# Five layer norms computed on two halves of the tokens, with the units around them split by half

## The chip, the cores and the metric

One core of a Trainium2 chip. The metric is the device time of one execution in microseconds (us). Engines: TensorE multiplies matrices into PSUM, VectorE and ScalarE work elementwise, GpSimd and SyncE issue most transfers (POOL and SP in the rows). Each engine runs its own queue in order; semaphores order the engines among each other.

## What is computed

One inference step of a decoder of 4 layers for 512 new prompt tokens and 8 sampled tokens, 1024 features wide. Layer 0 and 3 mix tokens by retention, layer 1 by pooling, layer 2 by sparse attention with an indexer. Each layer has two residual norms:

```
x = layer_norm(alpha * x + mixer(x))
x = layer_norm(alpha * x + swiglu(x))
layer_norm(x) = (x - mean) * rsqrt(var + 1e-5) * g + b        # mean and var over the 1024 features
swiglu(x)     = (silu(x @ w_a) * (x @ w_u)) @ w_out           # 2816 wide
```

## The kernel before

All 520 tokens stay on the chip with features on the partitions: `x` is 128 partitions by 8 chunks by 520 tokens. A unit is one block of 128 output features over all tokens. Its weights come from memory into one of four raw slots, ScalarE rounds them to a high part (`split_hi`, L445), VectorE takes the low part (`split_lo`, L455), and `multiply` (L471) sums three products (high by high, high by low, low by high) per 128 rows of depth, each for two halves of 260 tokens in two PSUM banks. There are two slots of split weights, so the split of unit k+2 waits until unit k is multiplied (`split_next`, L463), and two pairs of PSUM banks, so unit k+2 also waits until unit k is read out.

The stage list sets the order; each engine walks it with a program of its own. Ahead of each norm stands a stage that adds eight units to `x`: the output projection of retention (depth 4 chunks), of attention (`proj2`, depth 8) or the second part of the feed-forward output (`down..b`, depth 10). Per unit VectorE adds the product to `x`, ScalarE squares it (`square`, L950), VectorE adds value and square to two running sums (`add_up`, L1225).

The norm itself: on TensorE (L2378) mean by a product with a constant matrix (L2386), sums per token as single columns (L2392), and, after the root, a spread of 1/sd over all partitions (L2403); between them `hold` (L2372) multiplies an identity into a bank that nobody reads, 11, 10 and 13 times. On VectorE (L1812): subtract the mean (L1818), four small steps for the variance, reciprocal (L1835), scale (L1865), low part of the result (`x_lo`, L1207). On ScalarE (L1155): root (L1158), affine into `x` (L1164), high part `x_h` (L791). All of it goes chunk by chunk over all 520 tokens.

The next stage starts with two units interleaved, `multiply_first` (L500): it takes each chunk of `x_h` and `x_l` as it comes, with the second unit three chunks behind the first. Below these two are called the pair. Then the stage goes on with its third unit, called unit 2.

The norms are named by layer and place: norm0a is behind retention of layer 0, norm1b behind the feed-forward of layer 1, norm2a behind attention, norm2b behind the feed-forward of layer 2, norm3a behind retention of layer 3.

## Time and profile before

| | us |
|---|---|
| median of 3 runs (3249.36 to 3250.75) | 3249.58 |
| the profiled execution | 3249.74 |
| its span, first to last instruction | 3248.0 |
| TensorE matmul busy | 3083.2 (95%) |
| TensorE weight load busy | 2909.0 (90%) |
| VectorE busy | 1565.3 (48%) |
| ScalarE busy | 1031.9 (32%) |

Busy is the time in which an instruction of the engine was under way. Matmuls overlap each other, so the distance from one to the next, not the length of one, is what a matmul costs. A timeline row gives start, length, engine, line, operation, tiles and shapes; several instructions of one form in a row are merged, and the bracket at the end gives the idle time before and what ended it. A row of a windows view gives a stretch, its length, the busy time of each engine in it with the count of instructions, and the granted clock of TensorE as a share of 2.4 GHz.

### The profile page before, as it was taken

The page shows a single profiled execution, that of the slowest core. Times are in us where ns is not written, and L with a number is a line of the kernel's source. Part 1 is how long each engine was busy: PE and PEld are TensorE (multiplying, and loading weights), DVE is VectorE, ACT ScalarE, POOL GpSimd, SP SyncE. Part 2 cuts the span into 40 slices and gives each one's busy share as a digit, 9 for nine tenths or more (in the row PEclk, how much of TensorE's full clock was granted, in tenths as well). Part 3 has the DMA queues.
Part 4 walks back from the last instruction along what each step waited for, and adds up shares of the span by engine and source line. Part 5 has one row for each costly group of instructions (what it writes and reads, how often), then busy time and mean ns, then how long its engine had stood idle before and what let it go on. Part 6 is the DMA issues. An engine that isn't in the chain of part 4 may idle for free.

```text
span 3248.0 us, 55327 instructions
## 1 busy us (share of the span) xinstructions
PE 3083.2 (95%) x23519; PEld 2909.0 (90%) x23519; DVE 1565.3 (48%) x2423; ACT 1031.9 (32%) x1440; POOL 209.3 (6%) x342
## 2 busy tenths in 40 slices
PE   8999998999985999998898899999999999899998
PEld 7898896999985999997788799999989989699998
DVE  4555555432348332356986443234555555533234
ACT  3333332431224322232343143122523333332222
POOL 0111101000000000001011100000021011000000
PEclk9999998999996999999898899999999999899999
DMA  6444334232321332322122323233344443323231
GB/s 148 133 130 159 127 112 136 78 104 79 95 67 49 89 106 78 100 61 59 53 73 81 122 73 103 83 93 91 95 151 121 150 133 109 119 83 108 76 99 51
DMA packets 492389, 323.14 MB, mean 99 GB/s; under 512 B 29211, under 2 KB 468763, under 8 KB 492186
## 3 DMA queue, kind: packets, MB, share of 16 engines
q1 hardware_dynamic: 465394, 230.14, 24.9%
q0 software_dynamic: 26800, 90.18, 7.9%
q8 instruction: 150, 2.46, 0.3%
q14 instruction: 45, 0.37, 0.0%
HBM read 275.90 MB, written 44.82 MB: 99 GB/s over the span
## 4 chain that ended last, share of the span: by engine, by line
PE 88%; DVE 8%; ACT 2%; issue 2%; DMA 0%; POOL 0%; DVEq 0%; SPq 0%; ACTq 0%; POOLq 0%
PE ps L482 72%; PE ps L532 2%; PE ps L1900 2%; PE ps L513 2%; PE ps L533 2%; PE ps L534 2%; PE ps L2032 2%; DVE wf L1818 1%; DVE wf L1577 1%; PE ps L2022 1%; DVE tiny L1575 1%; DVE w_l L459 1%; ACT w_h L453 1%; DVE wf L1865 1%; PE ps L2336 1%
## 5 line engine op out<-in xcount | busy, mean ns | idle before, releaser
L482 PE MATMUL ps<-x_h,w_h 128*128 128x260 f32 x4576 | 936.0, 286 | 7.4 <-DVE w_l L459 5.2
L482 PE MATMUL ps<-x_h,w_l 128*128 128x260 f32 x4576 | 925.0, 284 | 0.0
L482 PE MATMUL ps<-x_l,w_h 128*128 128x260 f32 x4576 | 923.6, 284 | 0.0
L459 DVE TENSOR_TENSOR w_l<-w_raw,w_h 128x1024 fp32r<-128x1024 f32 (+3 forms) x440 | 527.9, 1200 | 817.0 <-ACT w_h L453 816.5
L453 ACT ACTIVATE w_h<-w_raw 128x1024 fp32r<-128x1024 f32 (+3 forms) x440 | 456.0, 1037 | 904.7 <-PE ps L482 874.5
L482 PEld LDWEIGHTS ps<-x_h,w_h 128*128 128x128 f32 x4576 | 710.0, 190 | 30.0 <-issue 23.7
L482 PEld LDWEIGHTS ps<-x_h,w_l 128*128 128x128 f32 x4576 | 708.6, 189 | 0.0
L482 PEld LDWEIGHTS ps<-x_l,w_h 128*128 128x128 f32 x4576 | 708.1, 189 | 0.0
L482 PE MATMUL ps<-rr,w_h 128*128 128x260 f32 x3968 | 639.4, 283 | 2.2 <-DVE w_l L459 1.1
L482 PEld LDWEIGHTS ps<-rr,w_h 128*128 128x128 f32 x3968 | 543.6, 188 | 4.1 <-issue 3.0
L482 PE MATMUL ps<-rr,w_l 128*128 128x260 f32 x1984 | 399.4, 283 | 0.0
L482 PEld LDWEIGHTS ps<-rr,w_l 128*128 128x128 f32 x1984 | 306.7, 189 | 0.0
L1790 DVE TENSOR_TENSOR wf<-ps,wf 128x520 f32<-128x520 f32 x88 | 61.5, 699 | 248.4 <-PE ps L482 248.4
L1117 ACT ACTIVATE wf<-ps 128x520 f32<-128x520 f32 x88 | 53.4, 606 | 343.7 <-PE ps L482 334.7
L532 PE MATMUL ps<-rr 128*128 128x512 f32 (+5 forms) x332 | 122.7, 372 | 7.4 <-DVE rr L1690 3.2
L1900 PE MATMUL ps<-ident,wf 128*128 128x128 f32 (+4 forms) x607 | 95.7, 290 | 35.5 <-DMA wf<-in_x_sample 9.5
L1804 DVE SCALAR_TENSOR_TENSOR x<-x,ps 128x520 f32<-128x520 f32 x40 | 27.9, 696 | 196.3 <-PE ps L482 196.3
L1900 PEld LDWEIGHTS ps<-ident,wf 128*128 128x128 f32 (+4 forms) x607 | 70.3, 142 | 56.7 <-issue 29.9
L533 PE MATMUL ps<-rr 128*128 128x512 f32 (+5 forms) x332 | 115.3, 349 | 0.0
L534 PE MATMUL ps<-rr 128*128 128x512 f32 (+5 forms) x332 | 115.1, 348 | 0.0
L1342 DVE SCALAR_TENSOR_TENSOR wf<-ps,wf 128x512 f32<-128x512 f32 x128 | 89.4, 743 | 2.5 <-ACT wf L856 2.5
L532 PEld LDWEIGHTS ps<-rr 128*128 128x128 f32 (+1 forms) x332 | 64.4, 195 | 27.6 <-issue 13.6
(278 smaller groups left out, 2765.6 us busy)
## 6 DMA issues: line engine op xcount, KB each, us to landing
w_raw<-in_ffn_w_in SPq DMA_DIRECT2D x176, 512.0 KB, 3.8
w_raw<-in_ret_w_in SPq DMA_DIRECT2D x96, 512.0 KB, 3.9
out<-wf POOLq DMA_DIRECT2D x72, 512.0 KB, 3.3
wf<-in_state_ret POOLq DMA_DIRECT2D x64, 512.0 KB, 5.6
w_raw<-in_ffn_w_out SPq DMA_DIRECT2D x32, 768.0 KB, 4.6
w_raw<-in_ffn_w_out SPq DMA_DIRECT2D x32, 640.0 KB, 4.2
w_raw<-in_ret_w_out SPq DMA_DIRECT2D x64, 256.0 KB, 2.9
w_raw<-in_dsa_w_in SPq DMA_DIRECT2D x27, 512.0 KB, 3.9
```

The costliest lines, as they stand in the source:

```text
L453: C.activation(whole(stage, k, w_h[:, n % 2, 0:m]), landed(stage, k, n, m), ACT.Copy).then_inc(S["w_hi"], 1)
L459: V.tensor_tensor(whole(stage, k, w_l[:, n % 2, 0:m]), landed(stage, k, n, m), whole(stage, k, w_h[:, n % 2, 0:m].bitcast(F32)), ALU.subtr ...
L482: mm = M.matmul(ps[:, 2 * (n % 2) + b, 0:HALF], lhs[:, c, :], rhs[:, c, cols], start=(c == 0 and term == 0), stop=(c == cs - 1 and term == 2))
L513: mm = M.matmul(ps[:, 2 * n + b, 0:HALF], lhs, rhs[:, c, cols], start=(c == 0 and term == 0), stop=(c == DC - 1 and term == 2))
L532: M.matmul(out, lhs_h, rhs_h, start=start, stop=False)
L533: M.matmul(out, lhs_h, rhs_l, start=False, stop=False)
L534: return M.matmul(out, lhs_l, rhs_h, start=False, stop=stop)
L1117: C.activation(halves(sil[:, q]), acc[0], ACT.Silu).then_inc(S["sil"], 1)
L1342: V.scalar_tensor_tensor(st[:, b % 4, d], ps[:, spread_bank(i, b), :], k_f[:, d, SEQ + b:SEQ + b + 1], st[:, b % 4, d], ALU.mult, ALU.add) ...
L1790: V.tensor_tensor(halves(h_raw[:, q]), acc[1], halves(sil[:, q]), ALU.mult).then_inc(S["h_raw"], 1)
L1900: return M.transpose(out, src, ident[0:n, 0:n])
L2032: mm = M.matmul(ps[32 * j:32 * j + 4, 6, :], qz[:, i % 2, d, g, j, :], st[:, (2 * g + j) % 4, d, :], start=(g + d == 0), stop=(g == NB // ...
```

## The change

For norm0a, norm1b, norm2a, norm2b and norm3a the norm works on two halves of 260 tokens (`norm_halves` on three engines), and it takes over the last two units of the stage ahead (units 6 and 7, counted in the eight) and the pair of the next stage.

- TensorE: unit 6 and unit 7 for the first half; unit 6 for the second half with the first half's statistics behind it or in its middle; unit 7 for the second half with the first half's spread in it or behind it; the pair for the first half, with the second half's statistics and spread between its chunks; the pair for the second half. In the pair the second unit is one group of two chunks behind the first. The `hold` products go.
- VectorE: adds and sums of units 6 and 7 by half; subtraction, scale and low part by half and two chunks at a time; the queue order is written out. The weight splits for the pair stand among the first half's steps, the second of them at their end.
- ScalarE: squares by half, two roots, per two chunks two affines into `x` and one copy into `x_h`.
- The stage ahead stops after six units, and the next stage begins with its third.

The diff, cut to its core (VectorE's and ScalarE's helpers and the semaphore counts are left out where a line of the text above says what they do):

```diff
+HALVED = {"norm0a": "sums0", "norm1b": "down1b", "norm2a": "proj2", "norm2b": "down2b", "norm3a": "sums3"}
+FOLLOWS = {"norm0a": "up0a", "norm1b": "idx2", "norm2a": "up2a", "norm2b": "ret3", "norm3a": "up3a"}
...
             def down(stage, last):
                 at = marks.here(stage)
-                for k in range(8):
+                for k in range(6 if stage in HALVED.values() else 8):
```

On ScalarE, `norm_halves`:

```diff
+                def affine(b, p):
+
+                    cols = prompt_halves()[b]
+                    act.wait_ge(*at("ln_e", 4 * b + p + 1))
+                    for c in (2 * p, 2 * p + 1):
+                        col = which * DC + c
+                        C.activation(x[:, c, cols], ln_e[:, c, cols], ACT.Identity, scale=lncol[:, 0, col:col + 1],
+                                     bias=lncol[:, 1, col:col + 1]).then_inc(S["x_n"], 1)
+                    act.wait_ge(*at("x_n", 8 * b + 2 * p + 2))
+                    C.activation(x_h[:, 2 * p:2 * p + 2, cols], x[:, 2 * p:2 * p + 2, cols], ACT.Copy
+                                 ).then_inc(S["x_hi"], 1)
+
+                square_half(6, 0)
+                square_half(7, 0)
+                if short:
+                    square_half(6, 1)
+                    split_next(split_hi, act, src, i, k - 1)
+                    root(0)
+                    square_half(7, 1)
+                    split_next(split_hi, act, src, i, k)
+                    for p in range(4):
+                        affine(0, p)
+                else:
+                    root(0)
+                    split_next(split_hi, act, src, i, k - 1)
+                    square_half(6, 1)
+                    for p in range(3):
+                        affine(0, p)
+                    square_half(7, 1)
+                    affine(0, 3)
+                    split_next(split_hi, act, src, i, k)
+                root(1)
+                for p in range(4):
+                    affine(1, p)
```

On VectorE, `norm_halves`:

```diff
+                add_half(6, 0)
+                sum_half(6, 0)
+                add_half(7, 0)
+                sum_half(7, 0)
+                if short:
+                    add_half(6, 1)
+                    sum_half(6, 1)
+                less_mean(0, 0)
+                less_mean(0, 1)
+                variance(0)
+                less_mean(0, 2)
+                inverse(0)
+                less_mean(0, 3)
+                if short:
+                    add_half(7, 1)
+                    sum_half(7, 1)
+                    split_next(split_lo, dve, src, i, k - 1)
+                    scale(0, 0)
+                    scale(0, 1)
+                    low(0, 0)
+                    scale(0, 2)
+                    low(0, 1)
+                    scale(0, 3)
+                    low(0, 2)
+                    low(0, 3)
+                    split_next(split_lo, dve, src, i, k)
+                else:
+                    add_half(6, 1)
+                    scale(0, 0)
+                    split_next(split_lo, dve, src, i, k - 1)
+                    scale(0, 1)
+                    low(0, 0)
+                    sum_half(6, 1)
+                    scale(0, 2)
+                    low(0, 1)
+                    scale(0, 3)
+                    add_half(7, 1)
+                    sum_half(7, 1)
+                    low(0, 2)
+                    low(0, 3)
+                    split_next(split_lo, dve, src, i, k)
+                less_mean(1, 0)
+                less_mean(1, 1)
+                variance(1)
+                less_mean(1, 2)
+                inverse(1)
+                less_mean(1, 3)
+                scale(1, 0)
+                scale(1, 1)
+                low(1, 0)
```

On TensorE, `norm_halves`:

```diff
+                def first_pairs(b, between):
+
+                    for p in range(4):
+                        if p in between:
+                            between[p](1)
+                        pe.wait_ge(*at("x_hi", 4 * b + p + 1))
+                        head(0, b, p, (0, 1))
+                        if p:
+                            pe.wait_ge(*at("x_lo", 4 * b + p))
+                            head(0, b, p - 1, (2,))
+                            head(1, b, p - 1, (0, 1, 2))
+                    pe.wait_ge(*at("x_lo", 4 * b + 4))
+                    head(0, b, 3, (2,))
+                    head(1, b, 3, (0, 1, 2))
+
+                short = cs == VC
+                stat_at, spread_at = (cs, cs) if short else (cs // 2, cs // 4)
+                tail(6, 0, range(cs))
+                tail(7, 0, range(cs))
+                tail(6, 1, range(stat_at))
+                stats(0)
+                if stat_at < cs:
+                    tail(6, 1, range(stat_at, cs))
+                tail(7, 1, range(spread_at))
+                spread(0)
+                if spread_at < cs:
+                    tail(7, 1, range(spread_at, cs))
+                first_pairs(0, {0: stats, 2: spread} if short else {1: stats, 3: spread})
+                first_pairs(1, {})
```

`short` is true behind retention (depth 4). `tail(m, b, part)` multiplies unit m for half b over the depth chunks in `part`; `head(m, b, p, terms)` multiplies unit m of the pair for half b and the chunk group p (two chunks), the terms being high by high, low weights by high, and high weights by low.

## Rows read from the trace of the kernel before

**Rows 1.** The page, part 1: busy us (share of the span) xinstructions of TensorE.

```profile
PE 3083.2 (95%) x23519; PEld 2909.0 (90%) x23519; DVE 1565.3 (48%) x2423; ACT 1031.9 (32%) x1440; POOL 209.3 (6%) x342
```

**Rows 2.** Windows, five norms: length, busy PE PEld DVE ACT POOL, PEclk, DMA, GB/s.

```profile
551.72:590.97 39.25, 33.39 (x214) 31.82 (x215) 27.08 (x45) 21.50 (x29) 0.00 (x0) 0.83 0.19 54
1416.66:1457.31 40.65, 38.76 (x288) 37.52 (x287) 26.01 (x42) 19.44 (x26) 0.79 (x2) 0.92 0.15 41
1865.28:1903.75 38.47, 34.53 (x265) 32.94 (x263) 26.71 (x43) 21.30 (x28) 0.00 (x0) 0.96 0.15 42
2258.17:2301.22 43.05, 38.83 (x289) 37.24 (x287) 26.84 (x42) 24.01 (x29) 4.71 (x7) 0.92 0.23 69
2814.71:2853.99 39.28, 33.37 (x214) 31.81 (x215) 27.09 (x45) 21.52 (x29) 0.00 (x0) 0.83 0.19 55
```

**Rows 3.** The chain that ended last, 1870 to 1906: start, length, what.

```profile
1869.90 7.09 PE ps L482 x59
```

**Rows 4.** Timeline of norm2a: mean, columns, subtractions, small step, root, spread, scale.

```profile
1878.49 1.15 PE L2386 MATMUL ps<-wf,avg 128*128 128x260 f32 x4 [0.21 <-DVE wf L1233]
1879.47 2.29 PE L2392 MATMUL ps<-avg,wf 128*128 128x1 f32 x20
1879.67 2.51 DVE L1818 TENSOR_TENSOR wf<-x,ps 128x520 f32<-128x520 f32 x4 [0.57 <-PE ps L2386]
...
1882.76 0.17 DVE L1833 TENSOR_SCALAR tiny<-tiny 128x5 f32<-128x5 f32 x1
1882.97 0.21 ACT L1158 ACTIVATE tiny<-tiny 128x5 f32<-128x5 f32 x1 [2.34 <-DVE tiny L1833]
...
1883.45 1.50 PE L2403 MATMUL ps<-ident,tiny 128*128 128x128 f32 x12 [0.40 <-DVE tiny L1835]
...
1885.02 0.69 DVE L1865 TENSOR_TENSOR wf<-wf,ps 128x520 f32<-128x520 f32 x1
```

**Rows 5.** Timeline of norm2a, ScalarE: affine, copy, next affine.

```profile
1892.00 0.81 ACT L1164 ACTIVATE x<-wf,lncol 128x520 f32<-128x520 f32 x1
...
1892.84 0.64 ACT L791 ACTIVATE x_h<-x 128x520 fp32r<-128x520 f32 x1
...
1893.47 0.82 ACT L1164 ACTIVATE x<-wf,lncol 128x520 f32<-128x520 f32 x1
```

**Rows 6.** Timeline behind norm2a: Silu of unit 0, splits for unit 2, unit 2.

```profile
1900.79 0.61 ACT L1117 ACTIVATE wf<-ps 128x520 f32<-128x520 f32 x1 [1.66 <-PE ps L513]
...
1901.29 1.05 ACT L453 ACTIVATE w_h<-w_raw 128x1024 fp32r<-128x1024 f32 x1
...
1902.38 1.23 DVE L459 TENSOR_TENSOR w_l<-w_raw,w_h 128x1024 fp32r<-128x1024 f32 x1 [3.81 <-ACT w_h L453]
...
1903.75 0.48 PE L482 MATMUL ps<-x_h,w_h 128*128 128x260 f32 x2 [0.83 <-DVE w_l L459]
```

**Rows 7.** Groups by form: xcount | busy us, mean ns | idle before.

```profile
L1294 DVE TENSOR_TENSOR rr<-wf,rr 128x256 fp32r<-128x256 f32 x8 | 3.4, 425 | 2.3 <-ACT rr L851 2.3
...
L1084 ACT ACTIVATE wf<-wf,tiny 128x512 f32<-128x512 f32 x8 | 5.8, 720 | 1.5 <-DVE tiny L1706 1.5
...
L1084 ACT ACTIVATE wf<-wf,tiny 128x256 f32<-128x256 f32 x8 | 4.1, 509 | 12.9 <-DVE tiny L1706 12.9
```

**Rows 8.** Timeline behind norm1b, the rotation of the index stage.

```profile
1457.31 1.04 PE L2147 MATMUL ps<-wf 128*128 128x260 f32 x4
```

**Rows 9.** Timeline of norm3a, VectorE adds unit 6.

```profile
2820.14 0.69 DVE L1455 TENSOR_TENSOR x<-ps,x 128x520 f32<-128x520 f32 x1
```

**Rows 10.** Windows of L513 alone in norm3a: length, busy PE PEld, PEclk, DMA, GB/s.

```profile
2841.00:2846.00 5.00, 5.00 (x24) 5.00 (x25) 0.50 0.00 0
```

**Rows 11.** Timeline of ScalarE from norm0b to norm1a: load, Square, Sqrt.

```profile
961.90 1.28 ACT L1158 ACT_TABLE_LOAD   x1
...
1035.30 0.64 ACT L955 ACTIVATE wf<-x 128x520 f32<-128x520 f32 x1 [1.38 <-DVE x L1486]
...
1041.20 0.21 ACT L1158 ACTIVATE tiny<-tiny 128x5 f32<-128x5 f32 x1 [5.26 <-DVE tiny L1833]
```

More of the change, by code:

```diff
@@ L156, in per @@
     def per(self, stage):
-        return {SHARED.get(n, n): per for n, per in PER[kind_of(stage)].items()}
+        return {SHARED.get(n, n): per for n, per in PER[counts_of(stage)].items()}
     def here(self, stage, i=0):
@@ L936, in project @@
                     last = i == RH - 1
-                    for k in range(12, 20):
+                    for k in range(12, 18 if last else 20):
                         if k == 19 and last:
@@ L944, in project @@
                             square(marks.here(sums(stage)), marks.here(stage, i), k - 13)
+                    if last:
+                        square(marks.here(sums(stage)), marks.here(stage, i), 5)
                 for i in range(RH):
@@ L1452, in project @@
                     last = i == RH - 1
-                    for k in range(12, 20):
+                    for k in range(12, 18 if last else 20):
                         dve.wait_ge(*unit_mark("mm", stage, i, k))
@@ L1798, in down @@
                 at = marks.here(stage)
-                for k in range(8):
+                for k in range(6 if stage in HALVED.values() else 8):
                     dve.wait_ge(*unit_mark("mm", stage, 0, k))
@@ L1893, in _ @@
                 elif kind == "norm":
-                    norm(stage)
+                    (norm_halves if stage in HALVED else norm)(stage)
         @block.tensor
@@ L2367, in down @@
                 multiply(pe, stage, 0, 0, h_h, h_l, cs, range(cs - 1, cs))
-                for k in range(1, 8):
+                for k in range(1, 6 if stage in HALVED.values() else 8):
                     pe.wait_ge(*(at("h_raw", 0) if k < 2 else at("z_add", k - 1)))
```

157 lines of the change are left out of this document (147 added, 10 removed).

## The prediction

> **What bounds the kernel now.** I read the page's busy shares first: TensorE has work in 95% of the span [rows 1], so time can only come from places where it runs something useless or waits. The windows around the five norms that the change touches show such places [rows 2]. Each window runs from the first matmul of the last-but-one unit ahead of the norm (unit 6; the last is unit 7) to the first matmul after the two units behind the norm (the pair; unit 2 comes next). The five add up to 200.7 us, 6% of the span. Matmuls of units 6 and 7 and of the pair cost 0.12 us each at full clock (59 in 7.09 [rows 3]). There are 12 per 128 rows of depth for units 6 and 7, and 96 for the pair: 17.3, 25.9, 23.0, 25.9 and 17.3 us, 109.4 in all. So 91 us are waits, statistics, filler matmuls and low clock. That is the pot, and the question is how much of it a norm in halves reaches.
>
> What ends last inside a window is the norm's own chain, in the timeline of norm2a [rows 4]: mean on TensorE, four subtractions, single-column sums, root, reciprocal, spread, scale, affine. After that ScalarE paces: one affine and one copy of a 520-wide chunk come every 1.47 us [rows 5], 11.8 for eight chunks, against 11.5 for the pair's 96 matmuls. At the end, unit 2 waits for Silu, a split on ScalarE and one on VectorE [rows 6].
>
> **Prices of the new pieces.** No instruction of before is 260 wide on these engines. VectorE: 256 columns take 0.425 [rows 7] against 0.69 for 520; consecutive ones step by 0.08 less, so 0.34. ScalarE: 512 to 256 columns saves 0.211 [rows 7], so the 0.82 affine becomes 0.60, step 0.50. A pair of chunks in one half is then two affines and one copy: 0.50 + 0.60 + 0.04 + 0.64 = 1.78 for the first, 1.68 after. Eight such groups are 13.5 us where 11.8 stood: ScalarE gets 1.7 us more per norm. The filler matmuls (34 a norm) go; they stood in waits, so that is nothing by itself, but see the clock below. TensorE's statistics become, per half, 0.45 mean, 1.35 for six columns, 0.8 spread: 5.2 for both, 4.8 before [rows 4]. VectorE's twelve half-wide adds are 4.1 where six of 0.61 were 3.7.
>
> **norm2a step by step**, time 0 being unit 6's first matmul, at full clock. Units 6 and 7 of the first half end at 5.9. Add, sum, square and sum follow until 7.2, when TensorE, half through unit 6 of the second half, comes to the mean. VectorE subtracts from 7.85: two subtractions 1.2, four small steps 0.8, a third subtraction ahead of the reciprocal: 10.7. TensorE reaches the spread after 18 more matmuls at 11.15; 12.05. Scale 0.7 and the first affine group 1.8: x_h at 14.55. The next three come at 16.3, 18.4 and 20.4 (1.68 each, plus waits for a weight split on VectorE and for the Square of unit 7).
>
> Now the point on which the forecast rests. On VectorE's queue the second half's first subtraction stands behind the first half's last low part and behind the split of the pair's second weights, which needs ScalarE's split (1.06), itself queued behind the last affine group. So: 20.4 + 1.06 + 1.2 = 22.5 with the waits. The halves do not overlap there; the second chain starts when the first is through. From 22.5: 1.2 + 0.8 + 0.6 (third subtraction) + 0.25 + 0.9 (spread) = 26.2, scale 0.7, four affine groups 6.8, the last x_h at 33.8. Twenty matmuls remain, 2.4, and 0.2 until the last is out: the pair ends at 36.4. Unit 0 of the pair ends only 6 matmuls before unit 1, where 18 lay between before, so Silu, split and split (0.5 + 1.06 + 1.22) stand open: unit 2 at 38.6. Before: 38.47. No gain, though 15 us of waits were there.
>
> **The other four.** For depth 10 (norm2b, norm1b), 18 more matmuls lie ahead of the spread, 2.16: unit 2 at 40.7 against 43.05 in norm2b, minus 2.3. In norm1b the rotation of the index stage follows at the pair's end, 38.6 against 40.65, but VectorE's work on it stands behind the split of unit 2, which lands 2.2 after the pair's end, where the rotation took 1.04 [rows 8]: minus 0.8. For depth 4 (norm0a, norm3a) VectorE is late already: it adds unit 6 of before at 5.4 after the window's start [rows 9]; the change saves about 1.0 there because the Square of unit 5 no longer stands behind a split. From 4.4: three groups of half add and two sums at 1.25 (8.1), two subtractions, small steps, two subtractions (11.4), a fourth group (12.7), a split 1.13, a scale 0.7, four affine groups 6.85 (21.4), low part 0.6, split 1.13: 23.1; plus the same 16.1: 39.2 against 39.25 and 39.28. Sum at full clock: 0 + 0.1 - 2.3 - 0.8 - 0.1 = -3.1, the gain chiefly in norm2b.
>
> **Added waits.** In the middle of the first half's pair TensorE waits for the sums of unit 7 (second half), behind which all further matmuls stand: 3.5 us idle at 15 to 18.6 in norm2a, as the Square sits behind three affine groups. Then 1.4 for the second split, then the second spread. All of that is covered, as the second chain is later still. Weight loads: SP issues when VectorE has split the slot before, at most 6 us later now, for a unit four places on, over 20 us off: nothing. POOL is not touched.
>
> **The clock.** Before loses to the 1.2 GHz level too (0.83 to 0.96 of the granted clock in the windows [rows 2]); in norm3a some 23 matmuls took 5.0 us, 0.217 each [rows 10]. Those losses are in the lengths that I compare with. After the change TensorE waits longest at 15 to 23, so I expect the low level there and after. Its price: the spread doubled, 0.6, and up to 32 matmuls until the second half at 0.097 more, 3.1, less the 0.7 to 2.2 of waits behind them; from 0 (all in a wait) to 3.0. With about half of the 32 at the low level and half of the waits used up it is 1.1; I take 1.1, times five, 5.5. Laid on norm2a as it stands, the same prices give 38.2 for 38.47: 0.2 short, times five, 1.0.
>
> Sum: -3.1 + 5.5 + 1.0 = +3.4. The profiled execution lasted 3249.74 (span 3248.0 plus 1.7 around it), 0.16 over the median of 3249.58. Forecast 3253.
>
> **A rule against the change.** Squares now run between two Sqrts. In the trace the Sqrt table was loaded at 961.90, Squares ran with it (1035.30), and the next Sqrt at 1041.20 needed no load [rows 11]; so I count one load a norm, as before. The Trainium skill (ScalarE: Activation LUTs, Table sets: the hidden batching unit) says that functions of different sets cost a load at each change, and names Square among no set's fillers; by that each norm would load twice more.
>
> **Rivals.** (1) The overlap works: VectorE is free for the second half when its statistics are out, at 20.6 instead of 22.5, and the clock stays up. Then -3.1 - 5 x 1.9 = -12.6, 3237. For it: the order by halves; against it: the queue order above, fixed in the code. 0.12. (2) Slower, over the clock: without filler and with waits of 3.5 and 1.4, the low level lasts into the second half's pair. There 12 matmuls at 0.217 make 2.6 per group where ScalarE brings one each 1.68, so 0.9 x 4 = 3.7 more per norm. It decides if the clock is still low when the second x_h comes, at 28. -3.1 + 5 x (1.1 + 3.7) + 1 = +22 if in all five, +11 if in two or three: 3261 to 3272. For it: norm3a's pair ran partly low [rows 10] although filler was there; against it: the pair itself keeps TensorE at 1.44 of 1.68 busy. 0.20. The Trainium skill (TensorE: Matmul & The Clock Gate, Why this matters for your kernels) asks for no idle gaps between bursts of matmuls, which is on this side. (3) Loads at each change between Square and Sqrt: two of 1.28 [rows 11] a norm, 12.8 in all, 3266. 0.03, given the row.
>
> **How the numbers follow.** A difference of 0.2% (6.5 us) is about what can be told from none. The forecast case, 0.65, spans its clock bounds (-3.1 to +13) and 2 us for the ScalarE price (0.1 on 20 groups): most of it lies between 3243 and 3256, 0.04 of it above. So same 0.61, slower 0.27 (with rivals 2 and 3), faster 0.12. The range 3241 to 3263 cuts off most of rival 1 and half of rival 2.
>
> **What would show it.** Right: windows of 38 to 42 us again, TensorE idle ahead of the second mean and of the second weights, VectorE's second-half subtraction directly behind a w_l split, ScalarE at 1.7 per group without gaps at the end, unit 2 waiting 2 us for w_l, five loads for Sqrt ahead of the five norms' first roots and none ahead of the second. Wrong: second-half subtractions that start before the first half's last low part; windows under 36 us; granted clock at its low level in the last 8 us of a window.

## The result, and the profile after

The changed kernel takes 3263.7 us (median of 6 runs, 3261.42 to 3264.85) where the kernel before took 3250.57 beside it (6 runs, 3249.36 to 3252.92): 1.0041 of it, 95% interval 1.003 to 1.0051. That is 13.1 us slower. The forecast was 3253, the range ended at 3263. The profiled execution has a span of 3262.7, so 14.7 more than before's 3248.0.

TensorE's work of the kernel after (the page, part 1, answers to [rows 1]): 12 us less, as filler is gone, in a longer span. The added time isn't work: it is waits, and matmuls issued at the lower clock.

```profile
PE 3070.9 (94%) x23369; PEld 2896.1 (89%) x23369; DVE 1572.6 (48%) x2478; ACT 1044.0 (32%) x1495; POOL 209.8 (6%) x342
```

The same five windows as [rows 2] in the kernel after, and under them the 10 us behind unit 2 of norm0a, norm2a, norm2b and norm3a (columns: stretch, length, busy us of PE, PEld, DVE, ACT, POOL with counts, PEclk, DMA share, GB/s):

```profile
552.06:593.33 41.27, 28.97 (x185) 26.76 (x185) 28.82 (x56) 24.09 (x40) 0.00 (x0) 0.79 0.17 52
1420.54:1459.75 39.21, 35.06 (x258) 33.75 (x256) 27.13 (x52) 20.96 (x37) 0.30 (x1) 0.91 0.16 41
1872.34:1911.97 39.63, 32.74 (x234) 31.07 (x233) 28.21 (x54) 23.96 (x39) 0.00 (x0) 0.91 0.14 41
2267.78:2312.57 44.79, 35.42 (x258) 33.66 (x257) 28.38 (x54) 26.96 (x40) 4.72 (x7) 0.91 0.20 63
2825.91:2866.90 40.99, 28.80 (x186) 26.61 (x185) 28.75 (x56) 24.09 (x40) 0.00 (x0) 0.79 0.18 52
...
593.33:603.33 10.00, 10.00 (x71) 10.00 (x72) 3.08 (x4) 2.19 (x3) 0.00 (x0) 0.83 0.37 107
1911.97:1921.97 10.00, 9.99 (x71) 10.00 (x72) 3.19 (x4) 2.19 (x3) 0.00 (x0) 0.84 0.37 107
2312.57:2322.57 10.00, 10.00 (x64) 10.00 (x65) 6.54 (x11) 2.62 (x3) 0.00 (x0) 0.73 0.73 221
2866.90:2876.90 10.00, 10.00 (x70) 10.00 (x71) 3.06 (x4) 2.19 (x3) 0.00 (x0) 0.83 0.37 107
```

The same view of the kernel before, behind its norm0a; its other three stretches also read x83 and 1.00:

```profile
590.97:600.97 10.00, 10.00 (x83) 10.00 (x84) 3.43 (x4) 2.45 (x4) 0.00 (x0) 1.00 0.35 105
```

Two sums come out of these rows.

- **The windows**: +2.02, -1.44, +1.16, +1.74, +1.71, that is +5.2. What norm1b gains is given back but for 0.3 right behind it: from unit 6 to the first matmul of the first index unit (L482 in the kernel before, L500 now) it is 46.23 us for 46.52. So +6.3. This one place isn't sharp: in a second run of the kernel after it is 47.73.
- **Behind the windows**: TensorE is busy all the time in each, but issues 71, 71, 64 and 70 matmuls in 10 us where it issued 83. At 0.12 each [rows 3] that is 1.4 + 1.4 + 2.3 + 1.6 = 6.7 us lost to the 1.2 GHz level, in stretches that before ran at 2.4 GHz throughout.

Together 13.0, where the medians differ by 13.1. The spans differ by 1.7 more, in places that the change doesn't touch: +3.0 in the attention between 1718 and 1842, -2.5 in the retention stage behind norm2b, and pieces of less than 0.4. The kernel before without its filler, below, shows nearly the same two there (+2.9 and -2.5), so they are not the halves'.

**What stands ahead of the low clock.** Timeline behind norm2a in the kernel after (start, us, engine, line, operation, count, idle time and its releaser; answers to [rows 6]):

```profile
1909.02 0.61 ACT L1137 ACTIVATE wf<-ps 128x520 f32<-128x520 f32 x1 [0.73 <-PE ps L2634]
...
1909.53 1.99 ACT L471 ACTIVATE w_h<-w_raw 128x1024 fp32r<-128x1024 f32 x2
...
1910.60 1.23 DVE L477 TENSOR_TENSOR w_l<-w_raw,w_h 128x1024 fp32r<-128x1024 f32 x1 [2.88 <-ACT w_h L471]
...
1911.97 0.56 PE L500 MATMUL ps<-x_h,w_h 128*128 128x260 f32 x1 [2.28 <-DVE w_l L477]
```

TensorE is idle for 2.28 us ahead of unit 2, where [rows 6] has 0.83. Norm0a and norm3a read 2.27. The forecast had this wait, for this reason and of this size; it didn't ask what follows it.

**Norm2b waits twice as long.** The same view there:

```profile
2305.96 3.68 ACT L824 ACTIVATE x<-x 128x4160 f32<-128x4160 f32 x1 [0.77 <-DVE x_l L1955]
...
2309.55 0.58 ACT L838 ACTIVATE wf<-ps 128x520 f32<-128x520 f32 x1
...
2312.57 0.56 PE L500 MATMUL ps<-x_h,w_h 128*128 128x260 f32 x1 [4.65 <-DVE w_l L477]
```

The retention stage behind norm2b begins on ScalarE with a pass over all of x (times ALPHA, 3.68 us). Unit 0's evacuation stands behind it. In the kernel before the pass stood there too:

```profile
2294.36 3.68 ACT L806 ACTIVATE x<-x 128x4160 f32<-128x4160 f32 x1 [0.77 <-DVE x_l L1207]
```

There it started 5.9 us ahead of the pair's end and ran beside the pair's matmuls, and unit 2 waited 0.94. Now ScalarE's last copy comes so late that the pass starts 2.0 us ahead of the pair's end.

### The profile page after: what moved, and what is told of

Same layout as the page of the kernel before. It is cut to its first block, busy times and chain, and to the rows that moved or that the text cites. A ratio compares the mean times of both kernels' runs of the same rounds, so it can differ in the third digit from the quotient of the medians.

```text
span 3262.7 us, 55172 instructions
## 1 busy us (share of the span) xinstructions
PE 3070.9 (94%) x23369; PEld 2896.1 (89%) x23369; DVE 1572.6 (48%) x2478; ACT 1044.0 (32%) x1495; POOL 209.8 (6%) x342
## 4 chain that ended last, share of the span: by engine, by line
PE 87%; DVE 7%; ACT 3%; issue 2%; DMA 0%; POOL 0%; DVEq 0%; SPq 0%; ACTq 0%; POOLq 0%
PE ps L500 70%; PE ps L550 2%; PE ps L551 2%; PE ps L552 2%; PE ps L2102 2%; PE ps L2234 2%; PE ps L2634 1%; DVE wf L1650 1%; PE ps L2224 1%; DVE tiny L1648 1%; DVE w_l L477 1%; ACT x L1199 1%; ACT w_h L471 1%; PE ps L531 1%; PE ps L2538 1%
## 5 line engine op out<-in xcount | busy, mean ns | idle before, releaser
L500 PE MATMUL ps<-x_h,w_h 128*128 128x260 f32 x4576 | 939.2, 287 | 14.7 <-DVE w_l L477 13.2
L500 PE MATMUL ps<-x_h,w_l 128*128 128x260 f32 x4576 | 927.6, 284 | 0.0
L500 PE MATMUL ps<-x_l,w_h 128*128 128x260 f32 x4576 | 926.3, 284 | 0.0
L500 PEld LDWEIGHTS ps<-x_h,w_h 128*128 128x128 f32 x4576 | 713.3, 190 | 37.6 <-issue 28.0
L500 PEld LDWEIGHTS ps<-x_h,w_l 128*128 128x128 f32 x4576 | 711.3, 190 | 0.0
L500 PEld LDWEIGHTS ps<-x_l,w_h 128*128 128x128 f32 x4576 | 710.8, 190 | 0.0
L500 PE MATMUL ps<-rr,w_h 128*128 128x260 f32 x3680 | 593.0, 283 | 1.8 <-DVE rr L1846 1.0
L500 PEld LDWEIGHTS ps<-rr,w_h 128*128 128x128 f32 x3680 | 504.4, 189 | 2.9 <-issue 1.9
L500 PE MATMUL ps<-rr,w_l 128*128 128x260 f32 x1840 | 370.5, 283 | 0.0
L500 PEld LDWEIGHTS ps<-rr,w_l 128*128 128x128 f32 x1840 | 284.6, 189 | 0.0
L550 PE MATMUL ps<-rr,w_h 128*128 128x260 f32 x240 | 75.1, 313 | 27.2 <-DVE rr L1595 20.5
```

The source lines that it names most:

```text
L500: mm = M.matmul(ps[:, 2 * (n % 2) + b, 0:HALF], lhs[:, c, :], rhs[:, c, cols], start=(c == 0 and term == 0), stop=(c == cs - 1 and term == 2))
L550: M.matmul(out, lhs_h, rhs_h, start=start, stop=False)
```

## Experiments

Ratios are to the kernel before, run on the same chip beside each, with their 95% interval. The kernel before had medians of 3248.7 to 3253.0 on these chips, so runs of different chips are compared by ratio. Three theories for the 13 us. **A**: the wait ahead of unit 2 lowers the clock behind the windows, and the ALPHA pass adds to it in norm2b. **C**: the queue order keeps the halves from overlapping, so there is no gain to set against any loss. The rivals: the clock falls for another reason (B), ScalarE's 13.5 us of affines set the windows whatever the order (D), the dropped filler makes the loss.

### The dropped filler by itself

```diff
-                held = stage not in ("norm0b", "norm3b")
+                held = stage in ("norm1a",)
```

> The kernel before, with the filler matmuls taken out of the five norms that the change touches and nothing else edited. It prices the filler by itself, which the change also drops. Theory A (the clock follows TensorE's idle stretches): each of the five norms gets 1 to 3 us longer through matmuls at 1.2 GHz in the pair or behind it, in all +5 to +13, 3256 to 3263, so that much of the change's loss would be the filler's and not the halves'. Rival B (filler standing in waits is worth nothing here): within 2 us of the kernel before, 3250.6.

Measured: 3256.1, ratio 1.0006 (0.9996 to 1.0016). Windows of norm0a and norm2b in this kernel (columns as above):

```profile
550.72:588.27 37.55, 29.35 (x180) 27.70 (x181) 27.07 (x45) 21.51 (x29) 0.00 (x0) 0.77 0.19 57
...
2264.05:2308.51 44.46, 36.16 (x255) 34.69 (x253) 26.96 (x43) 24.42 (x29) 4.71 (x7) 0.85 0.22 64
```

Norm0a and norm3a get 1.7 us shorter without filler, the other three 1.0 to 1.6 longer; the sum is 201.3 against 200.7 [rows 2]. By the ratio the filler is worth 2 us, and at most 5 (the upper end of the interval): most of the 13 isn't the filler's.

### Filler in the wait ahead of unit 2

```diff
                 first_pairs(1, {})
+                hold(20, 4)
```

> The kernel after, with 20 filler matmuls (256 columns, into a bank that is free by then) behind the second half's last matmul in each of the five norms, where TensorE otherwise stands idle for 2.3 us (4.6 in norm2b) ahead of unit 2. Theory A: that idle stretch is what makes the granted clock fall behind the windows. Then the 3.4 to 6.9 us at 1.2 GHz that follow the windows of norm0a, norm2a, norm2b and norm3a go, and with them about 1.5, 1.4, 2.4 and 1.5 us; the windows themselves stay within 0.5 us; in all about -6 against the kernel after, 3257. Rival B: the clock falls because of the waits inside the second half (mean, spread), and the fall only shows later. Then the stretches behind the windows stay and the time stays within 2 us of the kernel after's 3263.7, or rises where the filler delays unit 2.

Measured: 3259.95, ratio 1.0027 (1.0017 to 1.0037), so by the ratios 4.5 us of the 13.1 are back; 6 were expected. Behind norm2a and norm2b (norm0a and norm3a read x85 and 1.00 as norm2a does):

```profile
1908.95:1918.95 10.00, 10.00 (x85) 10.00 (x84) 3.44 (x4) 2.19 (x3) 0.00 (x0) 1.00 0.36 105
2307.63:2317.63 10.00, 10.00 (x70) 10.00 (x71) 7.38 (x11) 2.63 (x3) 0.00 (x0) 0.83 0.72 218
```

The low clock is gone behind three windows and less behind norm2b, where 20 matmuls cover only half of the 4.65 us. The windows' sum is 205.8 where it was 205.9. So theory A: what lowers the clock there is the idle time ahead of unit 2, not the waits further inside (B).

### The ALPHA pass moved behind the first evacuations

```diff
-                C.activation(x[:], x[:], ACT.Copy, scale=ALPHA).then_inc(S["xs"], 1)
+                def scale_x():
+                    C.activation(x[:], x[:], ACT.Copy, scale=ALPHA).then_inc(S["xs"], 1)
...
                     tail(1)
+                    if isinstance(i, int) and i == 0 and after_halves(stage):
+                        scale_x()
```

> The kernel after, with one edit in one stage: ScalarE's pass that scales all of x by alpha (128x4160, 3.7 us) in the stage behind norm2b runs after the first units' evacuations and splits on its queue, not ahead of them. Theory: this pass alone makes TensorE's 4.65 us of idle time ahead of unit 2 in norm2b, where the other four have 2.3. Then that gap falls to about 2.3 and the time by 2.4, to 3261.3 (up to 2 more if the clock stays up behind it). Rival: the gap stays because unit 2's second weights or its bank come late for another reason (a load, VectorE's split), and the time stays at 3263.7; or the pass, moved back, delays the adds of the following units by its 3.7 us and the gain is given back there.

Measured: 3261.97, ratio 1.003 (1.0019 to 1.0041). Norm2b's window, and from the timeline unit 2 behind it:

```profile
2267.88:2310.43 42.55, 35.39 (x258) 33.63 (x257) 28.37 (x54) 23.46 (x40) 4.13 (x7) 0.92 0.18 46
```

```profile
2310.43 0.47 PE L500 MATMUL ps<-x_h,w_h 128*128 128x260 f32 x2 [2.46 <-DVE w_l L477]
```

The window falls from 44.79 to 42.55 and the wait from 4.65 to 2.46, as the theory has it. The ratio is 0.0011 lower than the kernel after's and the intervals overlap, so the time alone couldn't tell this; the window can.

### Both together

The two edits above in one kernel.

> The kernel after with both of the earlier edits: 20 filler matmuls behind each second half's pair, and the alpha pass behind norm2b moved behind the first evacuations. Theory A with the alpha pass as the other missed term: the two terms add, about -5 (filler) and -3 (gap of norm2b, with the clock behind it), so the kernel comes to 3254 to 3257 where the kernel before has 3251 to 3253, that is the sum that the forecast made for the windows alone (+3.4), plus 1.5 at other places. Rival: the two overlap in norm2b (both act on the same idle time), and the time stays at hold_behind's 3260.

Measured: 3259.66 (3254.40 to 3263.07), ratio 1.0026 (1.0016 to 1.0037). The profile has norm2b's window at 41.93 and the others as with filler alone, and its execution took 3256.59, inside what was expected; the median didn't. The total leaves open whether the two add. A run without filler, further down, settles it with useful matmuls in the same wait.

### Unit 0 first: the same idle time given useful work

In the second half, unit 1's matmuls of the last three chunk pairs come behind all of unit 0's, so that 18 matmuls lie between the end of unit 0 and unit 2 where 6 lay.

```diff
                             head(0, b, p - 1, (2,))
-                            head(1, b, p - 1, (0, 1, 2))
+                            if b == 0 or p == 1:
+                                head(1, b, p - 1, (0, 1, 2))
                     pe.wait_ge(*at("x_lo", 4 * b + 4))
                     head(0, b, 3, (2,))
-                    head(1, b, 3, (0, 1, 2))
+                    for p in range(b, 4) if b else (3,):
+                        head(1, b, p, (0, 1, 2))
```

> The kernel after with one move on TensorE: in the second half, unit 1's matmuls of the last three chunk pairs come behind all of unit 0's, so that 18 matmuls (2.2 us) of useful work lie between the end of unit 0 and the start of unit 2 where 6 lay. No filler, nothing else. Unit 2 waits for Silu and two splits counted from the end of unit 0, so the windows stay within 0.5 us; what is tested is whether the idle time is what the clock behind the window answers to. Theory A: the wait ahead of unit 2 falls from 2.3 to about 0.8, and the 3.4 us at 1.2 GHz behind the windows of norm0a, norm2a and norm3a go, as with filler: -4 to -6 against the kernel after. Rival G: as much idle time now stands in small pieces inside the second half's pair, the clock falls there or behind as before, and the time stays within 2 us of the kernel after.

> The kernel after, unedited, beside the three others of this call, so that they can be compared with it on one chip. Expected: 3262 to 3266 where the kernel before has 3250 to 3253; the profile with the same windows as the first time within 0.5 us.

Measured: 3252.03, ratio 1.0007 (0.9998 to 1.0016); the unedited kernel after beside it 3262.17, ratio 1.0041 (1.0028 to 1.0055), with four windows within 0.2 us of the first time and norm1b's 1.5 longer. One move on one queue gives 10 us. The timeline behind norm2a, and under it the window of 10 us behind unit 2:

```profile
1902.44 0.60 ACT L1137 ACTIVATE wf<-ps 128x520 f32<-128x520 f32 x1
...
1905.40 0.47 PE L500 MATMUL ps<-x_h,w_h 128*128 128x260 f32 x2 [0.82 <-DVE w_l L477]
```

```profile
1905.40:1915.40 10.00, 10.00 (x83) 10.00 (x84) 3.43 (x4) 2.46 (x4) 0.00 (x0) 1.00 0.36 107
```

Silu no longer waits for TensorE (0.73 above), unit 2 waits 0.82, and the stretch behind is at full clock: x83 as before. So theory A holds with useful work in the gap as with filler, and rival G falls. The gain is larger than expected because four windows shrank too, by 0.5 to 1.6. In norm0a of the kernel after, TensorE ended the pair 4.3 us behind ScalarE's last copy of x, in norm2a 2.7, since its matmuls had run at 1.2 GHz until 583.9 and 1898.0; with unit 0 first, Silu stands behind fewer of these late matmuls.

Another part of the gain lies behind norm1b. The first 5 us of the first index unit there, in the kernel after and, under it, in this one:

```profile
1466.77:1471.77 5.00, 5.00 (x25) 4.90 (x24) 3.48 (x6) 0.64 (x1) 2.56 (x5) 0.54 0.53 140
...
1464.73:1469.73 5.00, 5.00 (x43) 4.97 (x42) 4.01 (x6) 0.74 (x2) 2.58 (x5) 1.00 0.54 141
```

That is 18 matmuls or 2.2 us. The kernel before loses this too (x26 and 0.57 there), so it is no part of the 13 us, and with filler behind the pair it was back as well (x42 and 1.00).

### Both moves, no filler

Unit 0 first, and the later ALPHA pass.

> The kernel after with two moves and no filler: unit 1's last matmuls behind unit 0's (as in the run of that move alone, 3252.0) and the alpha pass behind norm2b moved behind the first evacuations. Theory: the two missed terms are separate, so norm2b's wait ahead of unit 2, still 3.9 us in the run of the first move alone, falls to about 1, its window from 44.3 to 41.5, and the time by 2 to 4, to 3248 to 3250. Rival: the pass comes back as a delay of later evacuations, and the time stays at 3251 to 3253.

Measured: 3247.76, ratio 0.9984 (0.9975 to 0.9993). 3248 to 3250 was expected. By the ratio all of the 13 us are back, and 5 more. Windows (norm1b's to the start of the index stage's rotation; norm3a 39.75):

```profile
552.29:592.15 39.86, 29.02 (x186) 26.82 (x185) 28.84 (x56) 23.96 (x40) 0.00 (x0) 0.79 0.18 54
1417.56:1459.09 41.53, 36.70 (x259) 35.43 (x258) 27.61 (x53) 21.95 (x37) 0.56 (x1) 0.88 0.15 39
1865.77:1904.71 38.94, 32.83 (x234) 31.11 (x233) 28.22 (x54) 23.80 (x39) 0.00 (x0) 0.91 0.15 41
2259.12:2300.51 41.39, 35.56 (x258) 34.04 (x257) 28.34 (x53) 22.92 (x39) 3.44 (x6) 0.92 0.18 46
```

Norm2b went from 44.31 with the first move alone to 41.39, and the 10 us behind all four windows are at 1.00. The two terms are separate and add. Norm1b's row is longer than in the kernel after, but the first index unit starts 46.48 us after unit 6 (46.23 there) and runs at 1.00 (x43 in 5 us), where the kernel before runs at 0.57: this is part of the 5.

### Filler inside the windows

The filler behind the pair and the later ALPHA pass as above, and filler at the two longest waits:

```diff
+                    if b and not short:
+                        hold(24, 7)
                     pe.wait_ge(*at_s("sum_q", 8 + 2 * b))
...
+                    if b and short:
+                        hold(26, 4)
                     pe.wait_ge(*at("ln_rs", b + 1))
...
+                        if short and b == 0 and p == 0:
+                            hold(14, 4)
                         pe.wait_ge(*at("x_hi", 4 * b + p + 1))
```

> The kernel after with the filler behind the pair and the later alpha pass, and filler also in the two longest waits inside each window: 24 to 26 matmuls where TensorE waits for the second half's statistics (3.3 us) or spread (3.7 us in norm0a and norm3a), and 14 ahead of the first half's first x_h in norm0a and norm3a (2.0 us). The queue order is untouched. Theory A for the inside: the 6.8 to 17 us at 1.2 GHz inside each window (566.8 to 583.9 in norm0a) go or get shorter; norm0a and norm3a gain 1 to 2 us each, norm2a and norm2b 0.5 to 1, which were the forecast's clock term (1.1 a norm): 3 to 5 less than the kernel with the two outer edits alone, 3252 to 3256. Rival F (ScalarE's affines and copies pace the pair, so TensorE's clock inside is hidden): windows within 0.4 us, the time within 1.5 of that kernel's.

Measured: 3264.19, ratio 1.0043 (1.003 to 1.0057). The same places with 10, 14 and 8 matmuls, on the kernel with both moves and no filler behind the pair:

> The kernel of the run beside it, with filler in the waits inside the windows that fits them even at 1.2 GHz: 10 matmuls (2.2 us at 0.217) where TensorE waits 3.3 for the second half's squares in norm1b, norm2a and norm2b, 14 (3.0) where it waits 3.7 for the second spread in norm0a and norm3a, and 8 ahead of the first x_h there (1.7 of 2.0). Theory A for the inside: the second half's root comes no later than beside it (within 0.2 us of the window), the spells at 1.2 GHz inside get shorter, and norm0a and norm3a gain 1 us or more each, the rest 0.5: 3 to 4 less in all. Rival F (what ends last inside is ScalarE's and VectorE's chain, so TensorE's clock there is hidden and the forecast's term was counted for nothing): low spells shorter, windows within 0.4 us each, the time within 1.5.

Measured: 3258.43, ratio 1.0015 (1.0006 to 1.0024). Gains of 3 to 5 us were expected; both were slower than the kernels without this filler, and neither tells anything of the clock. Timeline of norm2a in the second:

```profile
1892.50 0.71 PE L2612 MATMUL ps<-wf,avg 128*128 128x260 f32 x2 [3.29 <-DVE wf L1916]
1892.86 2.22 PE L2584 MATMUL ps<-ident_r 128*128 128x256 f32 x10
1894.87 2.55 PE L2619 MATMUL ps<-avg,wf 128*128 128x1 f32 x12
```

The 3.29 us stand ahead of the mean, not behind it. The filler stood behind the wait and pushed the single-column sums back by its own 2 us. Ahead of the waiting instruction it looks like this (12 more stand ahead of the pair's second unit in norm0a and norm3a, and 8 ahead of the first x_h):

```diff
+                    if b and not short:
+                        hold(12, 7)
                     pe.wait_ge(*at_s("sum_s", 8 + 2 * b))
```

> The kernel of order_alpha with filler in the waits inside the windows, this time ahead of the waiting instruction: 12 matmuls ahead of the second half's mean in norm1b, norm2a and norm2b (3.3 us idle there), 8 ahead of the first x_h and 12 ahead of the pair's second unit in norm0a and norm3a (2.0 and 3.5 us idle). Each is at most 2.6 us long at 0.217. Theory A for the inside: the idle times are filled, the spells at 1.2 GHz inside the windows (17 us in norm0a and norm3a, 6.8 in the others) get shorter, norm0a and norm3a gain 1 us or more each, the others 0.5: 3 to 4 less than order_alpha's 0.9984 of the kernel before, 0.9973. Rival F (what ends last inside is VectorE's and ScalarE's chain, so the clock there is hidden): the idle times are filled, the windows stay within 0.4 us of order_alpha's, the time within 1.5.

Measured: 3251.65, ratio 0.9997 (0.9988 to 1.0006). In norm0a the filler is in the waits (the first 8 matmuls below, 12 more at 571.64), and under it stand the windows of norm0a and norm2a:

```profile
566.34 1.50 PE L2584 MATMUL ps<-ident_r 128*128 128x256 f32 x8
```

```profile
552.22:592.05 39.83, 32.06 (x205) 29.84 (x205) 28.82 (x56) 23.95 (x40) 0.00 (x0) 0.83 0.19 54
...
1868.75:1907.77 39.02, 34.36 (x246) 32.64 (x245) 28.18 (x54) 23.82 (x39) 0.00 (x0) 0.91 0.14 41
```

All windows are within 0.1 of the kernel without it, but for norm1b (0.56 shorter). The clock in norm0a rose from 0.79 to 0.83 for nothing: what ends last in the first half is VectorE's and ScalarE's chain. The 6.8 us at 1.2 GHz around the second spread (577.3 to 584.1 in norm0a) stayed in this run, so what they cost has not been measured. In norm2a the clock is 0.91 with the filler as without, so the run says nothing of norm2a.

Neither expectation held for the time: the ratio rose by 0.0013, though the intervals overlap. In the profiles 3.2 us of that lie between norm1b's first matmul and norm2a's (451.39 us for 448.21), because the low level is back behind norm1b:

```profile
1464.03:1469.03 5.00, 5.00 (x27) 4.90 (x26) 3.48 (x6) 0.64 (x1) 2.27 (x5) 0.59 0.48 132
```

### Another order for the two halves

The same instructions in another order on VectorE, ScalarE and TensorE, for each of the three depths. VectorE's queue for norm2a, in the names of the diff (add, sum, lm for less_mean, var, inv, sc for scale; slo is the split of w_l; then half and index):

```
after:   ... low 0 2; low 0 3; slo 1; lm 1 0; lm 1 1; var 1; lm 1 2; inv 1; lm 1 3; sc 1 0 ...
reorder: ... sum 7 1; low 0 0; slo 0; var 1; inv 1; slo 1; lm 1 0; lm 1 1; sc 1 0; low 0 1; sc 1 1; low 0 2; lm 1 2 ...
```

On ScalarE the second half's square, root and weight split stand between the first half's affines, and TensorE takes the second half's statistics and spread ahead of the first half's later matmuls. In the second half unit 1's last matmuls stand behind unit 0's, as in the run of that move alone.

> The kernel after, with the same instructions in the five norms in another order on VectorE, ScalarE and TensorE: the second half's adds, squares, statistics, subtractions and root are queued between the first half's scales and affines, and not behind the first half's last low part and the split of the pair's second weights. Nothing is added or left out. Theory C (the queue order serialises the two halves, which was the point on which the forecast rested): at full clock the windows shorten by 5 to 7 us each; with 1 to 2 us of low clock left in each, about -20 to -30 in all, 3234 to 3244. Rival D (ScalarE's 13.5 us of affines and copies per norm, or the clock, sets the windows whatever the order): windows within 1.5 us of those of the kernel after, the time within 6 of 3263.7.

Measured: 3223.61, ratio 0.9911 (0.9895 to 0.9928): 40 us under the kernel after, where 20 to 30 were expected. Windows of norm0a to norm2b (norm3a 32.12), and under them from norm2a's timeline VectorE's second-half subtraction and ScalarE's last first-half copy:

```profile
549.94:582.00 32.06, 26.04 (x185) 24.71 (x185) 27.79 (x56) 23.92 (x40) 0.00 (x0) 0.89 0.23 66
1407.43:1443.43 36.00, 34.70 (x259) 34.10 (x258) 27.15 (x53) 21.88 (x37) 0.74 (x2) 0.91 0.17 46
1856.00:1889.10 33.10, 30.75 (x234) 29.75 (x233) 27.58 (x54) 23.05 (x39) 0.00 (x0) 0.95 0.17 49
2243.51:2282.77 39.26, 34.71 (x258) 33.93 (x257) 27.93 (x54) 26.87 (x40) 4.72 (x7) 0.91 0.24 73
```

```profile
1875.86 1.29 DVE L1907 TENSOR_TENSOR wf<-x,ps 128x520 f32<-128x520 f32 x2
...
1877.30 0.64 ACT L1202 ACTIVATE x_h<-x 128x520 fp32r<-128x520 f32 x1
```

The subtraction starts 19.9 us into the window (22.3 in the kernel after) and ahead of the first half's last copy. ScalarE has the same affines and copies as in the kernel after: rival D falls.

One point put back, the one on which the forecast rested: VectorE's second chain again behind the first half's last low part, with ScalarE's root and TensorE's second spread moved to match.

> The reordered kernel with the one point put back on which the forecast rested: on VectorE the second half's chain (subtractions, variance, reciprocal) stands again behind the first half's last low part, and on ScalarE its root behind the first half's last affine pair; TensorE's second spread stands behind the first half's last matmul. Squares, adds, sums and weight splits stay where the reordered kernel has them. Theory C (this point serialises the halves): in the reordered norm2a the first half's last low part ends at 23.6 us of the window and the second half's first affine starts at 21.8; with the chain of 4.2 us (two subtractions, small steps, root, reciprocal, spread, scale) behind a low part that then ends at about 22.2, that affine starts at 26.4, so each window gets 4 to 5 us longer than the reordered kernel's (norm2a 33.1 to about 37.5, norm0a 32.1 to 36.5), in all +20 to +25 over 3223.6: 3244 to 3249. Rival E (what helped was the earlier weight splits, squares and adds): the windows stay within 1.5 us of the reordered kernel's, and the time within 6 of 3223.6.

Measured: 3253.16, ratio 1.0009 (1.0 to 1.0019). Norm0a and norm2a:

```profile
551.17:589.86 38.69, 29.43 (x185) 27.35 (x185) 28.16 (x56) 23.91 (x40) 0.00 (x0) 0.82 0.19 55
...
1867.95:1906.69 38.74, 33.71 (x235) 31.92 (x233) 27.81 (x53) 22.94 (x38) 0.00 (x0) 0.87 0.14 42
```

Each window is 4.1 to 6.6 us longer, 29.6 in all, which is the whole difference in time. So this point, and not the earlier squares or splits, serialises the halves (rival E falls). I had expected 4 to 5 each; the low level came back inside (0.89 to 0.82 in norm0a). The other 10 of the 40 us are about what unit 0 first gave alone, and both kernels here have that move; they weren't tested apart.

### What beats both kernels

The other order with the later ALPHA pass:

> The reordered kernel with the alpha pass behind norm2b moved behind the first evacuations. Theory: the pass is the last thing that makes unit 2 wait in norm2b of the reordered kernel (3.26 us of TensorE's time idle there, 0.1 to 0.9 in norm0a, norm2a and norm3a); the gap falls to about 0.8 and the 3.4 us at 1.2 GHz behind it go too, so 2.4 to 4 less than the reordered kernel, 3219.5 to 3221. Rival: as in the kernel after, the window gains 2.2 but the time only 1 to 2, for the pass comes back as a delay of later evacuations: 3222 to 3223.

Measured: 3221.19, ratio 0.9914 (0.9897 to 0.9931); norm2b's window 37.0 where the reordered kernel has 39.3, as expected. The same with filler in norm0a and norm3a:

```diff
+                    if cs == VC and b == 0 and p == 0:
+                        pe.wait_ge(*at_s("z_half", 1))
+                        hold(12, 2 * (slot_of(to, 0, 0) % 2))
                     pe.wait_ge(*at("x_hi", 4 * b + p + 1))
```

> The same as the run beside it (reordered, alpha pass later), with 12 filler matmuls in norm0a and norm3a in the 2.7 us in which TensorE waits for the first half's first x_h. Theory A (TensorE's idle time ahead is what lowers the clock): the 6.8 us at 1.2 GHz that follow there (563.9 to 570.7 and 2809.9 to 2816.7 in the reordered kernel) go or get shorter, and each of the two norms gains 1 to 2 us of the up to 3.4 that they cost: 2 to 4 less than the run beside it. Rival: the fall comes from the single-column statistics and spread, in which TensorE shows as busy, and filler in the wait changes nothing; or the filler itself runs at 1.2 GHz (0.22 us each, 2.6 in all) and pushes the first half's matmuls back by up to 1: 0 to +2.

Measured: 3218.68, ratio 0.9907 (0.989 to 0.9924): 32 us under the kernel before. Norm0a's clock is 1.00 in this run, 0.89 in the run beside it, and the window 32.07 where it is 32.10: a second place in which the clock inside costs nothing. So the gain that was expected there didn't come. The medians do differ by 2.5, within both intervals; in the profiles 1.2 of it are norm2b's (35.78 for 37.00), where nothing was added. And with more filler in all five:

```diff
+                    if b:
+                        hold({4: 3, 8: 10, 10: 8}[cs], 7)
                     pe.wait_ge(*at_s("sum_q", 8 + 2 * b))
```

> The reordered kernel with the later alpha pass and the 12 filler matmuls at norm0a and norm3a, and with 3, 8 or 10 more (by the depth of the unit) in the wait for the second half's squares, 0.6 to 1.5 us long, in all five norms. Theory A: the 3.4 to 6.8 us at 1.2 GHz that are left inside norm1b and norm2b (1429.0 to 1435.9 and 2261.9 to 2265.3) go, and 1 to 2 us with them: 3216 to 3218 where the kernel without these had 3218.7. Rival: no change, or up to 1 slower because filler that is under way holds back the statistics.

Measured: 3220.08, ratio 0.9909 (0.9895 to 0.9923): nothing gained. This filler stands behind the mean as well, and norm2a's window got 1.2 longer (34.30).

## Why the prediction was wrong, point by point

**The order of the halves: right.** VectorE's second-half subtraction stands directly behind the first half's last low part and the split of w_l. Timeline of norm2a in the kernel after:

```profile
1892.55 0.70 DVE L1955 TENSOR_TENSOR x_l<-x,x_h 128x520 fp32r<-128x520 f32 x1 [0.62 <-ACT x_h L1202]
...
1893.50 1.23 DVE L477 TENSOR_TENSOR w_l<-w_raw,w_h 128x1024 fp32r<-128x1024 f32 x1 [0.25 <-ACT w_h L471]
...
1894.64 1.30 DVE L1921 TENSOR_TENSOR wf<-x,ps 128x520 f32<-128x520 f32 x2
```

Counted from 1872.34, x_h of the first half is out at 14.4, 16.1, 18.2 and 20.2 (forecast 14.55, 16.3, 18.4, 20.4), the subtraction starts at 22.3 (22.5), the last x_h is out at 34.7 (33.8), unit 2 starts at 39.6 (38.6 at full clock, 39.9 with the clock terms). Order and half-wide prices were worked out correctly from rows of another width.

**The windows: right but for norm2b.** Forecast with 1.3 of clock terms each: 40.5, 39.9, 39.9, 42.0 and 40.5 (norm0a, norm1b's pair end, norm2a, norm2b, norm3a). Measured: 41.3, 39.2, 39.6, 44.8, 41.0. **The first failing step is norm2b**, taken over from norm2a by adding 18 matmuls: what follows it was not looked up. Its successor puts a pass of 3.68 us on ScalarE between the norm and unit 0's evacuation. It cost 2.4 us directly (unit 2 waits 4.65 for 2.28) and about 0.8 more behind (64 matmuls for 71).

**The second failing step is the end of the sum.** The forecast priced the wait ahead of unit 2 by its length and laid the clock's price inside the windows only, with nothing behind them. Behind them the level fell for 6.7 us' worth, half of the loss (the 0.8 of norm2b is in it). The sum closes with these two: 3.4 forecast, 2.4 for the pass, 6.7 behind the windows make 12.5 of the 13.1. The clock section of the prediction asked what waits inside a window do to the matmuls behind them, and didn't ask the same of the wait that it had itself put at the end.

**The clock inside: about the right size.** The forecast had 1.3 a norm over the chain at full clock. In the kernel after the windows end 2.1 (norm0a), 0.6 (norm1b's pair), 1.0 (norm2a) and 1.8 (norm3a) above that chain, and norm2b 1.9 with the pass moved (42.55 for 40.7): 1.5 on average, though no run isolates how much of it is the clock's. For norm2a the rows show the path. The second half's reciprocal is out at 1897.3, but TensorE is still in the first half's matmuls, which ran at 1.2 GHz from 1891.2 to 1898.0. So the spread comes 1.5 us later, and VectorE's scale waits for it:

```profile
1897.12 0.17 DVE L1940 RECIPROCAL tiny<-tiny 128x3 f32<-128x3 f32 x1
...
1898.75 0.72 PE L2618 MATMUL ps<-ident,tiny 128*128 128x128 f32 x6
...
1899.51 1.30 DVE L1948 TENSOR_TENSOR wf<-wf,ps 128x520 f32<-128x520 f32 x2 [1.64 <-PE ps L2618]
```

In norm0a the loss comes at the end, in the 4.3 us of late matmuls. Ahead of the second spread the run with filler in the waits shows no cost there; what the spread itself costs at the low level is open. With both moves and no filler the windows are only 0.3 to 0.7 above the chain, but this isn't the clock's price: with unit 0 first the chain's end is shorter too, as Silu no longer waits 0.73 us for TensorE.

**The rivals.** (2), slower over the clock at 3261 to 3272, holds the measured time but not by its mechanism: the second half's pair didn't run low to its end (0.96 to 1.00 in the last 8 us ahead of its end in the four norms), the units behind it did. The Trainium skill (TensorE: Matmul & The Clock Gate, Why this matters for your kernels) warns of idle gaps between bursts of matmuls; I quoted it for this rival and not against my own gap of 2.2 us. The gaps that the page speaks of are longer than that one, and the measurement decides: behind 2.27 and 2.28 us of idle time the granted clock reads 0.83 and 0.84, behind 0.82 it reads 1.00. (1), the overlap, needs another order; then it gives far more than the 12.6 forecast for it, because the second chain starts earlier and, but for norm2b, unit 2 hardly waits (0.1 to 0.9 us). (3) fell, as the row had said. ScalarE in norm2a of the kernel after:

```profile
1879.20 1.28 ACT L1191 ACT_TABLE_LOAD   x1
1882.21 0.21 ACT L1191 ACTIVATE tiny<-tiny 128x3 f32<-128x3 f32 x1 [1.73 <-DVE tiny L1935]
...
1883.92 0.40 ACT L1186 ACTIVATE wf<-x 128x260 f32<-128x260 f32 x1
...
1896.64 0.21 ACT L1191 ACTIVATE tiny<-tiny 128x3 f32<-128x3 f32 x1 [3.18 <-DVE tiny L1935]
```

One load ahead of the first root, Squares and affines behind it, and a second root with none; over the five norms there are five loads for ten roots. The Trainium skill (ScalarE: Activation LUTs, Table sets: the hidden batching unit) names Square among no set's fillers, by which two more loads a norm would stand here; the rows show none, and the measurement decides.

**Still open**: what the 6.8 us of low clock around each second spread cost by themselves, and why the attention took 2 to 3.7 us less in the profiled execution of the kernel before than in those of all the others.

## What to carry to other kernels

Splitting a stage into halves gave little here (5 us at best) as long as the second half's chain was queued behind the first half's last steps; the same instructions in another order were worth 40 us, and putting one point back cost 30. Cost a wait of TensorE twice, by its length and by the clock behind it, and end the sum only where the clock is up again; if useful matmuls can stand in the wait, put them there first (10 us by moving unit 1's behind unit 0's, part of it inside the windows). When a stage ends later on another engine than before, read the successor's first instructions on that engine: what was hidden stands in the open.

## What the runs showed that I had not expected

A wait of 2.3 us cost 1.4 to 1.6 us more behind it here, through 12 or 13 matmuls fewer in 10 us in which TensorE shows as busy throughout; no idle time in any view shows this loss, only the counts and the granted clock do. And low clock may cost nothing: norm0a's window is 32.1 at 0.89 as at 1.00, where another engine's chain ends last. In norm2a of the kernel after it did cost, as the second spread stood behind slow matmuls on TensorE's queue.
